# Four transformer layers in one kernel: where masks, forget rows, a table's spread and halves of tokens stand

## Chip, cores, metric

The kernel runs on one core of a Trainium2 chip. The metric is the device time in microseconds of one execution, median of three runs.

## The reference

512 tokens of width 1024 pass through a first block of two layers, then a second block of two layers; all is fp32. Cut to what matters here:

```python
# first block, each of 2 layers: h = x @ w_in, split into four branches
y_mla = causal attention of rms-normed, projected q and kv, with rope
y_sb  = stick breaking: A[t,s] = sigmoid(z) * prod_{s<j<t} (1 - sigmoid(z[t,j])), s < t only
y_fox = causal attention, logit[t,s] += c[t] - c[s], c = cumsum(log_sigmoid(forget))
y_mem = softmax attention over x's queries and a memory of 256 rows
merged = sum_n sigmoid(merge) * (branch_n * silu(gate_n)) @ w_branch[n]
x = layer_norm(alpha * x + merged @ w_out)
# second block, each of 2 layers: h = rms_norm(x); z = h @ w_in, four branches
A: q, k rms-normed per head, axial rope, full attention    B: rope, window of 128, sinks
C: neighbourhood attention with a table of biases (rpb)    D: rope, softmax1 - lam * softmax2, rms norm
x = x + (concat of branches * silu(gates)) @ w_out ; at the end rms_norm
```

## The kernel before

`plan()` runs when the program is built. It makes one list of steps (`put(kind, ...)`), and each of the five engine programs walks this list and executes the steps that concern it, so every engine's queue is in order and an instruction that waits holds all behind it. The planner sets the order: `alongside()` interleaves the attention of one branch (scores, turns by TensorE, products) with the projections ("fill") of the next, by estimates of their cost. Stages of a layer in the first block: mem, mla, sb, fox, merge and output, layer norm; in the second block: A, B, D, C, output, rms norm.

A matrix product in fp32 is three matmuls on parts of the operands (`xh,wl`, L1399; `xl,wh`, L1400; `xh,wh`, L1401): activations and weights are split into a high half, a cast on ScalarE (ACT), and a low half, a subtraction on VectorE (DVE) or GpSimd (POOL). `wload()` puts a weight's load on SyncE (SP), 1 MB or in pieces, double buffered: load j waits for the casts of j-2. `hold` in the planner's state delays casts of weights. ACT casts it (L1552), DVE (L1897) and POOL (L2300) make the low half in turn. Activations enter a layer token-major in four tiles of 128 tokens; `features()` turns a tile by TensorE (L1362) and ACT (L1563) and DVE (L1904) split it. `opened()` runs the first projection in two halves of 256 tokens, with the turn of tiles 2 and 3 between, so that the first half needs tiles 0 and 1 only.

Names that the change touches: `spread` writes the C branch's bias table (`zscr` in HBM, two DMAs of 1920 KB, L1577 on ACT), which `bias` reads much later and whose DMA the sticks step waits for as well; `normed` is the rms norm of mla's compressed q and kv (result on DVE, high half on ACT in L1653, low half on POOL); `sticks` on DVE is a scan (L2166), a mask of the diagonal block (L2169) and a product (L2172), twice per step; `foxrow` are two DVE instructions per head (L2035) that add the decay rows to fox's q and k; `newton` refines a reciprocal root in four small instructions (L1870 to L1876), `newton_wide` one of 128x512 (L1860 to L1866); `dmix` combines D's two softmaxes (L2151, L2153, L2156); `tabs` are the rope tables that SP loads (L2416) for the rope of A, B and D (L2212). `out_partial` (wo2a) is the output projection of three branches, the fill of the C stage: 4 weights x 4 tiles x 6 x 3 = 288 matmuls of 256 columns; `sum` after it adds the last branch (wo2b).

## Time and profile before

| what | value |
| --- | --- |
| three runs, us | 1534.04, 1537.66, 1539.85; median 1537.66 |
| the profiled execution's own time | 1534.89 us |
| its span, first to last instruction | 1533.1 us, TensorE clock granted 0.975 of full |
| busy: TensorE / VectorE / ScalarE / GpSimd | 92% / 57% / 46% / 24% |
| chain of work that ended last | PE 69%, DVE 17%, ACT 8% |

PE is the TensorE matmul, PEld its weight load; a "q" behind an engine's name is its queue, where DMAs are issued. "L12" is line 12 of the kernel. A bracket behind an instruction is the engine's idle time before it and what ended it. A granted clock of 1.00 is 2.4 GHz, 0.50 is 1.2 GHz.

### The profile page before, as it was taken

What the parts mean: (1) busy time and instruction counts of PE and PEld (TensorE: products, weight loads), DVE (VectorE), ACT (ScalarE), POOL (GpSimd) and SP (SyncE); (2) the same over time, 40 slices, a digit from 0 to 9 for tenths busy, and PEclk for the clock granted to TensorE, in tenths of its full rate; (3) what the DMA queues carried; (4) which work ended last, traced back from release to release, by engine and by line L of the source; (5) the groups of instructions that cost most, each with busy time, mean ns of one, the idle gap of its engine ahead of it and who ended that gap; (6) DMA issues with size and microseconds to landing.
All of it is one profiled execution on the core that took longest, in us unless ns stands there. A gap on an engine that the chain in (4) does not pass through costs nothing.

```text
span 1533.1 us, 21207 instructions
## 1 busy us (share of the span) xinstructions
PE 1413.1 (92%) x8026; PEld 1091.0 (71%) x8026; DVE 869.9 (57%) x1657; ACT 709.6 (46%) x1525; POOL 366.7 (24%) x265
## 2 busy tenths in 40 slices
PE   7999899999989999999997899988998899988997
PEld 6767576777977677777786766665776766665776
DVE  4555337467662553465577565457656465557655
ACT  3555345455234554455543454445444344445443
POOL 2232131245231322223541112320111112320111
PEclk9999999999999999999998899998999899998999
DMA  6413620225242221112263232511313332411311
GB/s 227 111 30 87 158 83 15 78 67 213 97 151 56 52 88 56 55 45 62 91 214 98 60 77 48 111 56 49 97 62 111 83 76 53 99 55 49 97 63 55
DMA packets 191121, 131.73 MB, mean 86 GB/s; under 512 B 91436, under 2 KB 181164, under 8 KB 191020
## 3 DMA queue, kind: packets, MB, share of 16 engines
q1 hardware_dynamic: 179534, 112.29, 26.3%
q10 hardware_dynamic: 11486, 18.09, 3.7%
q8 instruction: 64, 1.05, 0.3%
q14 instruction: 37, 0.30, 0.1%
HBM read 118.03 MB, written 12.32 MB: 85 GB/s over the span
## 4 chain that ended last, share of the span: by engine, by line
PE 69%; DVE 17%; ACT 8%; issue 3%; DMA 1%; ACTq 1%; POOL 0%; DVEq 0%; POOLq 0%
PE pb L1399 18%; PE pb L1400 16%; PE pb L1401 16%; PE pb L1477 6%; PE pb L1421 5%; PE pb L1455 4%; ACT prob L1533 3%; ACT wh L1552 2%; ACT tmp L1533 1%; DVE wl L1897 1%; DVE small L2143 1%; DVE prob L2156 1%; DVE xl L1904 1%; DVE scr L2166 1%; DMA wr<-w_out 1%
## 5 line engine op out<-in xcount | busy, mean ns | idle before, releaser
L2300 POOL TENSOR_TENSOR wl<-wr,wh 128x512 fp32r<-128x512 f32 x170 | 236.4, 1390 | 886.2 <-ACT wh L1552 882.8
L1399 PE MATMUL pb<-xh,wl 128*128 128x512 f32 (+1 forms) x832 | 350.9, 422 | 25.5 <-DVE xl L1904 21.9
L1400 PE MATMUL pb<-xl,wh 128*128 128x512 f32 (+1 forms) x832 | 321.7, 387 | 0.0
L1401 PE MATMUL pb<-xh,wh 128*128 128x512 f32 (+1 forms) x832 | 321.7, 387 | 0.0
L1897 DVE TENSOR_TENSOR wl<-wr,wh 128x512 fp32r<-128x512 f32 x200 | 161.1, 807 | 198.7 <-ACT wh L1552 198.4
L1399 PEld LDWEIGHTS pb<-xh,wl 128*128 128x128 f32 x832 | 162.0, 195 | 103.7 <-issue 50.1
L1552 ACT CAST wh<-wr 128x512 fp32r<-128x512 f32 x370 | 211.1, 603 | 29.3 <-PE pb L1401 23.8
L1401 PEld LDWEIGHTS pb<-xh,wh 128*128 128x128 f32 x832 | 161.7, 194 | 31.7
L1400 PEld LDWEIGHTS pb<-xl,wh 128*128 128x128 f32 x832 | 162.4, 195 | 24.3 <-issue 3.8
L1533 ACT ACTIVATE prob<-prob,small 128x512 f32<-128x512 f32 (+3 forms) x128 | 76.3, 596 | 148.5 <-DVE small L2120 139.1
L1455 PE MATMUL pb<-cst,prob 128*128 128x128 f32 x768 | 120.8, 279 | 22.3 <-ACT prob L1533 8.4
L1399 PE MATMUL pb<-wh,xl 128*128 128x256 f32 x448 | 130.0, 290 | 8.0 <-DVE xl L2062 3.5
L1455 PEld LDWEIGHTS pb<-cst,prob 128*128 128x128 f32 x768 | 95.2, 143 | 54.3 <-issue 14.6
L1400 PE MATMUL pb<-wl,xh 128*128 128x256 f32 x448 | 126.7, 283 | 0.0
L1401 PE MATMUL pb<-wh,xh 128*128 128x256 f32 x448 | 126.7, 283 | 0.0
L1533 ACT ACTIVATE tmp<-pb,cst 128x512 f32<-128x512 f32 (+3 forms) x128 | 82.6, 645 | 71.2 <-PE pb L1421 21.4
L1533 ACT ACTIVATE prob<-pb,small 128x512 f32<-128x512 f32 (+1 forms) x96 | 58.4, 611 | 111.4 <-DVE small L2107 57.8
L1399 PEld LDWEIGHTS pb<-wh,xl 128*128 128x128 f32 x448 | 85.7, 191 | 13.0 <-DVE xl L2062 4.3
L1780 ACT COPY prob<-pb 128x512 f32<-128x512 f32 (+3 forms) x128 | 61.4, 480 | 69.3 <-PE pb L1455 68.3
L1399 PE MATMUL pb<-wh,yl 128*128 128x256 f32 (+1 forms) x272 | 87.4, 321 | 2.5 <-DVE wl L1897 1.3
L2180 DVE COPY prob<-pb 128x512 f32<-128x512 f32 (+3 forms) x128 | 70.5, 551 | 31.3 <-PE pb L1455 30.8
L1400 PEld LDWEIGHTS pb<-wl,xh 128*128 128x128 f32 x448 | 85.8, 192 | 0.7 <-issue 0.5
(196 smaller groups left out, 2446.5 us busy)
## 6 DMA issues: line engine op xcount, KB each, us to landing
wr<-w_in SPq DMA_DIRECT2D x39, 1024.0 KB, 5.1
wr<-w_in SPq DMA_DIRECT2D x48, 256.0 KB, 4.6
wr<-w_out SPq DMA_DIRECT2D x10, 1024.0 KB, 6.4
wr<-w_branch SPq DMA_DIRECT2D x48, 128.0 KB, 2.3
x<-prob SPq DMA_DIRECT2D x12, 512.0 KB, 2.6
wr<-w_out SPq DMA_DIRECT2D x48, 128.0 KB, 2.9
wr<-w_mem_kv SPq DMA_DIRECT2D x4, 1024.0 KB, 5.6
prob<-x ACTq DMA_DIRECT2D x2, 2048.0 KB, 10.2
```

Of the source, the lines that this page charges most:

```text
L1399: e.matmul(ps, ll, rh, start=start, stop=False)
L1400: e.matmul(ps, lh, rl, start=False, stop=False)
L1401: t = e.matmul(ps, lh, rh, start=False, stop=stop)
L1421: t = e.matmul(bank(b)[:, 0:128 * (hi - lo)], lhs, rhs, start=True, stop=br != "mla")
L1455: t = e.transpose(bank(b)[:, c], probs(p)[:, c], C("ident"))
L1477: t = e.matmul(bank(b)[64 * half:64 * half + 64, lo:hi], v_[:, j, vc:vc + 64], turns(s["t"][half])[:, j, lo - 256 * ih:hi - 256 * ih], sta ...
L1533: return e.activation(o, i, f, bias=C("zero", 0, i.shape[0]) if bias is None else bias, scale=scale, **kw)
L1552: e.copy(wh[:, j % 2, c0:c1], wr[:, j % 2, c0:c1]).then_inc(w_hi.sem, w_hi.mark((j, c)))
L1780: t = e.copy(turns(t_)[:, lo:hi, 128 * i:128 * i + 128], bank(b)[:, 0:128 * (hi - lo)].rearrange("p (j c) -> p j c", c=128))
L1897: t = e.tensor_tensor(wl[:, j % 2, c0:c1], wr[:, j % 2, c0:c1], wh[:, j % 2, c0:c1].bitcast(F32), ALU.subtract)
L2180: t = e.tensor_copy(turns(t_)[:, lo:hi, 128 * i:128 * i + 128], bank(b)[:, 0:128 * (hi - lo)].rearrange("p (j c) -> p j c", c=128))
L2300: t = e.tensor_tensor(wl[:, j % 2, c0:c1], wr[:, j % 2, c0:c1], wh[:, j % 2, c0:c1].bitcast(F32), ALU.subtract)
```

## The change

1. The table's spread moves from ACT to SP and is split into eight DMAs of 15 rows, two behind each of the next four weight loads of layer 0's mla stage.
2. The sb scores' diagonal block gets its strict mask as a matmul (identity times a matrix of large negative numbers) that adds to the scores; DVE's L2169 and the mask in the scan go. Two 128x128 tiles for it are made once.
3. `foxrow` moves from DVE to ACT.
4. The high and low halves of the `normed` rows become a step of their own, `normhi`, put about 5 us of the planner's time later.
5. Layer 1 of the first block opens with halves too: only tile 3 is turned between them.
6. Each layer of the second block opens with the first halves of two weights, Ag and Aq, then tiles 2 and 3, then Ag's and Aq's second halves.
7. Of the output projection wo2a, tiles 2 and 3 of its last weight (36 matmuls of 256 columns) are left and run between the sums of tiles 1 and 2.
8. `newton` has three instructions and its first does not wait for ACT's root; `newton_wide` has three; `dmix` does both halves' small instructions in one and waits for both exps first.

On ACT's queue in layer 0's mla stage, before (`ls` is the lambda step, `prob` the scores, `wr`/`wh` a weight and its high half, `zscr` the table):

```order
L1533 ACTIVATE u<-pb,cst 128x512
L1533 ACTIVATE ls<-ls,cst 128x4
L1577 DMA zscr<-scr 3840x1x128 x2
L1533 ACTIVATE prob,small<-prob,small 128x512 x2
L1552 CAST wh<-wr 128x512 x2
L1780 COPY prob<-pb 128x3x128
```

And on SP's queue in the changed kernel, from the load of the small tables on:

```order
L2442 DMA scr<-rpb_c 60x31 x2
L2410 DMA wr<-w_in 128x8x256
L2448 DMA zscr<-scr 960x1x128 x2
L2410 DMA wr<-w_in 128x8x256
L2448 DMA zscr<-scr 960x1x128 x2
L2410 DMA wr<-w_in 128x8x256
L2448 DMA zscr<-scr 960x1x128 x2
L2410 DMA wr<-w_in 128x8x256
L2448 DMA zscr<-scr 960x1x128 x2
L2410 DMA wr<-w_in 128x8x256
```

Between the lambda's exp and the scores' exps nothing stands on ACT any more; SP, which had five loads in a row there, has two parts after each of the first four.

On ACT in the mem stage of layer 0, where the normed rows of q and kv (`setB`) are cast; before:

```order
L1533 ACTIVATE tmp<-setB,cst 128x512
L1653 CAST yh<-setB 128x512 x3
L1533 ACTIVATE prob,small<-pb,small 128x256 x2
L1552 CAST wh<-wr 128x512 x2
L1780 COPY prob<-pb 128x2x128
L1533 ACTIVATE tmp<-pb,cst 128x512
L1533 ACTIVATE tmp<-tmp,cst 128x512
L1533 ACTIVATE prob,small<-pb,small 128x256 x2
L1653 CAST yh<-setB 128x512 x2
L1780 COPY prob<-pb 128x2x128
```

And now:

```order
L1585 ACTIVATE tmp<-setB,cst 128x512
L1585 ACTIVATE prob,small<-pb,small 128x256 x2
L1604 CAST wh<-wr 128x512 x2
L1837 COPY prob<-pb 128x2x128
L1700 CAST yh<-setB 128x512 x3
L1585 ACTIVATE tmp<-pb,cst 128x512
L1585 ACTIVATE tmp<-tmp,cst 128x512
L1585 ACTIVATE prob,small<-pb,small 128x256 x2
L1837 COPY prob<-pb 128x2x128
L1604 CAST wh<-wr 128x512 x2
L1700 CAST yh<-setB 128x512 x2
```

The casts of the three q rows and of the two kv rows now stand behind the copies of the turned scores.

On SP at the second block's beginning (`x<-prob` stores a tile, 128x8x64 is a quarter of a weight); before:

```order
L2365 DMA wr<-w_in 128x8x64 x4
L2416 DMA tabs<-tables 128x512 x2
L2365 DMA wr<-w_in 128x8x64 x4
L2365 DMA wr<-w_in 128x8x256
```

And now:

```order
L2410 DMA wr<-w_in 128x8x64 x8
L2466 DMA tabs<-tables 128x512 x2
L2410 DMA wr<-w_in 128x8x256
L2410 DMA wr<-w_in 128x8x64 x4
```

The rope tables stand behind four more pieces of a weight than before.

The diff, the planner's part:

```diff
+            spread(2)
+    def spread(n):
+        for _ in range(n):
+            if st["spread"] in range(8):
+                put("spread", l=st["spread"] // 4, r=15 * (st["spread"] % 4))
+                st["spread"] += 1
...
+    def halves(w, ep, half, held):
+        for c in range(2):
+            drain(gemm("fm", w, 128 * c, 128 * c + 128, ("x", ep), range(8), n=256, b=held[c], off=256 * half,
+                       end=half == 1))
...
+        halves(w, ep, 0, held)
+        between()
+        halves(w, ep, 1, held)
...
+            ready = now() + 5000
+            for _ in range(40):
+                if now() < ready:
+                    yield
+            put("normhi", l=l, grp=grp)
...
+        rest_of(norm_q)
...
+        rest_of(norm_kv)
...
-        if l:
-            held = [drain(gemm("fm", w, 128 * c, 128 * c + 128, ("x", l), range(8))) for c in range(2)]
-        else:
-            held = opened(w, l, lambda: last_features(l, *X))
+        held = opened(w, l, lambda: last_features(l, X, (3,) if l else (2, 3)))
...
+            st["spread"] = 0
...
+            yield from proj_fm("sbq", l, "sb", "q", l, False)
             if l == 0:
                 put("lambdas")
-                put("spread")
-            yield from proj_fm("sbq", l, "sb", "q", l, False)
...
+        spread(8)
...
-            for turned in ((0, 1), (2,), (3,), ()):
+            for turned in ((0, 1), (2,), ()):
                 next(parts)
                 advance_late(late)
                 for i in turned:
                     run(features(1, i, (X[i],)))
             rest_of(parts)
-            give(*X)
+            while advance_late(late):
+                pass
...
-        for x in gate(br + "g", ep, br, l, (lambda: last_features(ep)) if br == "A" else None):
+        two, held = [None, None], [(), ()]
+        if br == "A":
+            two, held = [wnext(br + "g"), wnext(br + "q")], [[GR[0].take() for _ in range(2)] for _ in range(2)]
+            st["hold"] = True
+            for w, h in zip(two, held):
+                halves(w, ep, 0, h)
+            last_features(ep)
+            halves(two[0], ep, 1, held[0])
+        for x in gate(br + "g", ep, br, l, two[0], held[0]):
             if x is not None:
                 box["u"] = x
             yield
+        if br == "A":
+            st["hold"] = False
+            halves(two[1], ep, 1, held[1])
...
+        w = two[1] if br == "A" else wnext(br + "q")
...
+            if br == "A" and n < 2:
+                b = held[1][n]
+            else:
+                b = yield from beside(gemm("fm", w, c0, c0 + 128, ("x", ep), range(8)))
...
-            sq = TM.take() if br == "A" else None
+            sq = TA.take() if br == "A" else None
...
-            for i in range(4):
+            for i in range(2 if m == 3 else 4):
                 b = yield from gemm("tok", w, 0, 256, ("y2", l), range(4 if i in held else 0, 6), tile=i, b=held.get(i),
                                     start=i not in held)
                 put("acc", l=l, m=m, i=i, b=b)
                 give(b)
                 yield
-            wdone(w)
+            if m < 3:
+                wdone(w)
+        box["w"] = w
+    def out_left(l, w, i):
+        b = drain(gemm("tok", w, 0, 256, ("y2", l), range(6), tile=i))
+        put("acc", l=l, m=3, i=i, b=b)
+        give(b)
...
+        st["hold"] = True
...
+            if i == 2:
+                for n in (2, 3):
+                    out_left(l, box["w"], n)
+                    advance_late(late)
+                wdone(box["w"])
+                st["hold"] = False
...
```

TensorE's, ScalarE's and VectorE's parts (the code of `spread` and `foxrow` is otherwise what it was; SP now runs `e.dma_start(zscr[l][r], src)` for 15 rows `r`):

```diff
                         lhs, rhs = q_[:, 2 * c + half, ti], k_[:, 2 * c + half, tk]
                     else:
                         lhs, rhs = q_[r, c, ti], k_[r, c, tk]
-                    t = e.matmul(bank(b)[:, 0:128 * (hi - lo)], lhs, rhs, start=True, stop=br != "mla")
-                    if br != "mla":
+                    t = e.matmul(bank(b)[:, 0:128 * (hi - lo)], lhs, rhs, start=True, stop=br not in ("mla", "sb"))
+                    if br not in ("mla", "sb"):
+                        t.then_inc(logit.sem, logit.mark(b))
+                if br == "sb":
+                    w.wait_ge(v_fn, v_fn.at("masks"))
+                    for b in s["b"]:
+                        t = e.matmul(bank(b)[:, 128 * i:128 * i + 128], identr[:, :], strict[:, :], start=False, stop=True)
                         t.then_inc(logit.sem, logit.mark(b))
...
-            elif k == "spread":
-                for l in range(2):
-                    w.wait_ge(d_z, d_z.at("z"))
-                    src = zrow[:, l, :].unsqueeze(1).to_broadcast([60, 64, P])
-                    e.dma_start(zscr[l], src).then_inc(d_spread.sem, d_spread.mark("z"))
...
-            elif k == "normed":
+            elif k == "normhi":
...
+            elif k == "foxrow":
+                l, h = s["l"], s["h"]
+                w.wait_ge(v_fn, v_fn.at(("foxsum", l)))
+                w.wait_ge(p_fn, p_fn.at(("zeros", l)))
+                fa, fb = CONST_COLS["foxa"][0], CONST_COLS["foxb"][0]
+                p0 = 64 * (1 - h % 2)
+                for dst, n in ((QKV["fox"][0], 0), (QKV["fox"][1], 1 + h)):
+                    t = act(dst[p0:p0 + 36, h, :], fz[:, :], ACT.Identity, cst[0:36, fa + n:fa + n + 1],
+                            cst[0:36, fb + n:fb + n + 1])
+                    t.then_inc(a_copy.sem, a_copy.mark(("foxrow", l, h)))
...
             for g, n in tn.free():
                 w.wait_ge(g, n)
-            e.tensor_tensor(x, o, o, ALU.mult).then_inc(v_fn.sem, v_fn.mark())
+            e.scalar_tensor_tensor(x, v, dim * 1e-6, o, ALU.add, ALU.mult).then_inc(v_fn.sem, v_fn.mark())
             w.wait_ge(v_fn, v_fn.n)
-            e.scalar_tensor_tensor(x, v, dim * 1e-6, x, ALU.add, ALU.mult).then_inc(v_fn.sem, v_fn.mark())
+            e.scalar_tensor_tensor(x, x, -0.5 / dim, o, ALU.mult, ALU.mult).then_inc(v_fn.sem, v_fn.mark())
             w.wait_ge(v_fn, v_fn.n)
-            e.tensor_scalar(x, x, -0.5 / dim, 1.5, ALU.mult, ALU.add).then_inc(v_fn.sem, v_fn.mark())
+            e.scalar_tensor_tensor(o, x, 1.5, o, ALU.add, ALU.mult).then_inc(v_fn.sem, v_fn.mark(*key, ends=(tn,)))
             w.wait_ge(v_fn, v_fn.n)
-            e.tensor_tensor(o, o, x, ALU.mult).then_inc(v_fn.sem, v_fn.mark(*key, ends=(tn,)))
-            w.wait_ge(v_fn, v_fn.n)
-
-        def newton(rs, var, scale, eps, x, y):
-            e.tensor_scalar(y, var, scale, eps, ALU.mult, ALU.add).then_inc(v_fn.sem, v_fn.mark())
+        def newton(rs, var, scale, eps, x, y, root):
+            e.tensor_scalar(y, var, -0.5 * scale, -0.5 * eps, ALU.mult, ALU.add).then_inc(v_fn.sem, v_fn.mark())
+            w.wait_ge(a_fn, a_fn.at(root))
             w.wait_ge(v_fn, v_fn.n)
             e.scalar_tensor_tensor(x, rs, y, rs, ALU.mult, ALU.mult).then_inc(v_fn.sem, v_fn.mark())
             w.wait_ge(v_fn, v_fn.n)
-            e.tensor_scalar(x, x, -0.5, 1.5, ALU.mult, ALU.add).then_inc(v_fn.sem, v_fn.mark())
-            w.wait_ge(v_fn, v_fn.n)
...
                     t.then_inc(v_att.sem, v_att.mark(("max", b)))
             elif k == "dmix":
                 l, i = s["l"], s["i"]
+                first, ratio = (small[:, s["sm"].slot.i, c + i:c + i + 5:4] for c in (8, 24))
+                for use in s["ta"]:
+                    w.wait_ge(a_att, a_att.at(("exp", use)))
+                e.reciprocal(ratio, ratio).then_inc(v_att.sem, v_att.mark())
+                w.wait_ge(v_att, v_att.n)
+                t = e.scalar_tensor_tensor(ratio, ratio, lam[:, l:l + 1], first, ALU.mult, ALU.mult)
+                t.then_inc(v_att.sem, v_att.mark())
+                w.wait_ge(v_att, v_att.n)
                 for half in range(2):
-                    d, x, p, use = probs(s["e"][half]), 4 * half + i, s["e"][half], s["ta"][half]
-                    ratio = sm(s["sm"], 24 + x)
-                    w.wait_ge(a_att, a_att.at(("exp", use)))
-                    e.reciprocal(ratio, ratio).then_inc(v_att.sem, v_att.mark())
-                    w.wait_ge(v_att, v_att.n)
-                    t = e.scalar_tensor_tensor(ratio, ratio, lam[:, l:l + 1], sm(s["sm"], 8 + x), ALU.mult, ALU.mult)
-                    t.then_inc(v_att.sem, v_att.mark())
-                    w.wait_ge(v_att, v_att.n)
-                    t = e.scalar_tensor_tensor(d, tm(use), ratio, d, ALU.mult, ALU.add)
+                    d, p, use = probs(s["e"][half]), s["e"][half], s["ta"][half]
+                    t = e.scalar_tensor_tensor(d, tm(use), sm(s["sm"], 24 + 4 * half + i), d, ALU.mult, ALU.add)
                     t.then_inc(v_att.sem, v_att.mark(("mixed", p), ends=(use,)))
             elif k == "sticks":
                 n = 128 * (s["i"] + 1)
                 for p, use in zip(s["e"], s["ta"]):
                     w.wait_ge(d_spread, d_spread.at("z"))
-                    x, lo, d, dg = tm(use)[:, 0:n], tmpz[:, 0:n], probs(p)[:, 0:n], slice(n - 128, n)
+                    x, lo, d = tm(use)[:, 0:n], tmpz[:, 0:n], probs(p)[:, 0:n]
                     w.wait_ge(a_att, a_att.at(("keep", use)))
                     w.wait_ge(v_att, v_att.n)
-                    m = mask_cols("after", 512 - n, 512)
-                    t = e.tensor_tensor_scan(lo[:, ::-1], x[:, ::-1], m[:, ::-1], 1.0, ALU.mult, ALU.max)
+                    t = e.tensor_tensor_scan(lo[:, ::-1], x[:, ::-1], x[:, ::-1], 1.0, ALU.mult, ALU.bypass)
                     t.then_inc(v_att.sem, v_att.mark(ends=(use,)))
                     w.wait_ge(a_att, a_att.at(("break", p)))
-                    t = e.scalar_tensor_tensor(d[:, dg], mask_cols("after", 384, 512), 1.0, d[:, dg], ALU.is_lt, ALU.mult)
...
```

## Rows read from the trace of the kernel before

**Rows 1.** The page, part 1: busy us, share and instructions by engine.

```profile
PE 1413.1 (92%) x8026; PEld 1091.0 (71%) x8026; DVE 869.9 (57%) x1657; ACT 709.6 (46%) x1525; POOL 366.7 (24%) x265
```

**Rows 2.** Timeline of PE: start, us, instruction; brackets are idle before, and releaser.

```profile
109.94 1.08 PE L1477 MATMUL pb<-prob,tbias 128*64 128x256 f32 x8 [2.10 <-ACT prob L1780]
...
169.32 1.11 PE L1455 MATMUL pb<-cst,prob 128*128 128x128 f32 x4 [5.21 <-DVE prob L2180]
...
443.17 1.97 PE L1362 MATMUL pb<-cst,prob 128*128 128x128 f32 x8 [4.25 <-DVE prob L2087]
...
837.17 1.97 PE L1362 MATMUL pb<-cst,setB 128*128 128x128 f32 x8 [7.20 <-DVE stats L1870]
844.56 0.58 PE L1399 MATMUL pb<-xh,wl 128*128 128x256 f32 x1 [5.42 <-DVE xl L1904]
...
858.42 0.39 PE L1399 MATMUL pb<-xh,wl 128*128 128x256 f32 x1 [4.35 <-DVE xl L1904]
...
1191.55 0.58 PE L1399 MATMUL pb<-xh,wl 128*128 128x256 f32 x1 [8.36 <-DVE xl L1904]
```

**Rows 3.** Windows: length; PE, PEld, DVE, ACT, POOL busy; clock, DMA share, GB/s.

```profile
165.90:172.70 6.80, 3.38 (x10) 2.79 (x11) 3.17 (x9) 4.28 (x12) 1.27 (x1) 0.50 0.94 190
442.40:449.20 6.80, 6.03 (x28) 6.03 (x29) 2.69 (x4) 2.21 (x4) 1.28 (x1) 0.50 0.20 79
858.80:862.20 3.40, 3.40 (x19) 3.40 (x18) 0.00 (x0) 0.00 (x0) 0.00 (x0) 0.50 1.33 226
848.60:851.80 3.20, 3.20 (x28) 3.20 (x28) 1.15 (x5) 3.13 (x7) 0.15 (x1) 1.00 0.41 164
```

**Rows 4.** Timeline of ACT and its queue (ACTq) in layer 0's mla stage.

```profile
156.52 9.47 ACTq L1577 DMA_DIRECT2D zscr<-scr  x2
166.04 0.72 ACT L1533 ACTIVATE prob<-prob,small 128x512 f32<-128x512 f32 x1 [9.23 <-issue]
```

**Rows 5.** DMA: list of issues; line L1577 alone; timelines of SP's queue and ACT.

```profile
wr<-w_in SPq DMA_DIRECT2D x39, 1024.0 KB, 5.1
...
DMA to landing us min/median/max: 13.8/18.3/22.7
...
199.07 9.97 SPq L2365 DMA_DIRECT2D wr<-w_in  x2
...
213.62 1.14 ACT L1552 CAST wh<-wr 128x512 fp32r<-128x512 f32 x2
```

**Rows 6.** Lines L2169 and L2035: ns min, median, max; first and last start.

```profile
L2169 DVE SCALAR_TENSOR_TENSOR prob<-cst,prob x32: 254/267/1296, 221.2 to 675.1; 128x128 f32<-128x128 f32 x32
...
L2035 DVE TENSOR_SCALAR setA<-fz,cst x16: 530/532/1475, 234.5 to 669.9; 36x512 f32<-36x512 f32 x16
```

**Rows 7.** Waits of PE, 225 to 246: us in total, times, longest.

```profile
PE pb L1455 <- DVE prob L2172: 3.2, 3, 1.3
```

**Rows 8.** Timeline of PE in layer 0's D stage: eight 128x128 turns.

```profile
1030.50 1.03 PE L1455 MATMUL pb<-cst,prob 128*128 128x128 f32 x8
```

**Rows 9.** Timeline of the tail: PE's last matmul, DVE's last Newton step and product.

```profile
1523.82 0.39 PE L1401 MATMUL pb<-wh,yh 128*128 128x512 f32 x1
...
1527.89 0.15 DVE L1870 TENSOR_SCALAR stats<-stats 128x1 f32<-128x1 f32 x1
...
1528.71 1.28 DVE L2095 SCALAR_TENSOR_TENSOR prob<-prob,stats,scr 128x1024 f32<-128x1024 f32 x1
```

**Rows 10.** Timelines of SP's queue and DVE at the second block's start.

```profile
856.00 2.96 SPq L2365 DMA_DIRECT2D wr<-w_in  x4
859.01 1.61 SPq L2416 DMA_DIRECT2D tabs<-tables  x2
...
875.02 0.69 DVE L2212 TENSOR_TENSOR tmp<-pb,tabs 128x512 f32<-128x512 f32 x1 [0.99 <-PE pb L1508]
```

**Rows 11.** Windows, columns as in group 3: D stage, C stage.

```profile
1025.00:1050.00 25.00, 20.05 (x112) 13.23 (x105) 19.98 (x42) 13.01 (x34) 2.29 (x2) 0.93 0.14 43
...
1125.00:1150.00 25.00, 25.00 (x189) 19.74 (x185) 13.37 (x32) 11.04 (x25) 3.53 (x3) 1.00 0.12 43
```

61 lines of the change are left out of this document (25 added, 36 removed).

## The prediction

> **What bounds the kernel now.** I read the page's busy shares first. TensorE (PE) works 1413.1 of 1533.1 us, 92%, and no other engine comes near [rows 1]. So the kernel ends when PE's matmuls end, and a change can move the time in three ways only: by closing gaps in front of PE, by giving PE its higher clock (2.4 GHz) in a stretch where it had the lower (1.2 GHz), or by changing the number of PE's instructions. Next I read PE's timeline for bracketed idle times. Outside PE's busy time lie 1533.1 - 1413.1 = 120 us; the reader is to see in [rows 2] that the long ones stand at few places: after a two-layer block's or layer's beginning (443, 837, 844, 858, 1191), once in the mla stage of layer 0 (169), once in the mem stage (110), and then each names the engine that ended it. Then I read the granted clock over stretches [rows 3]: each long gap is followed by a stretch at 0.50, the lower level; so a gap costs its own length and then as much again as half of PE's busy time in the slow stretch. In 165.9 to 172.7, PE was busy 3.38 us at half clock, so 1.7 us were lost to the clock; in 442.4 to 449.2 it was 6.03, so 3.0; three other stretches (from 111.3, 230.8 and 858.8) are 3.40 long and full, 1.7 each, of which the last stands in the rows.
>
> The sum is made against the profiled execution's own 1534.9 us (a span of 1533.1), which stands 2.8 below the median of 1537.66. I take the sum off the median at the end. "Layer" numbers below are those of the kernel: two blocks with layers 0 and 1 each.
>
> **1. The table's spread leaves ScalarE.** ACT issued two DMAs that took its queue 9.47 us, and the exp that the softmax of the mla stage wanted stood behind them, idle 9.23 [rows 4]. PE's gap of 5.21 at 169.32 hangs on it: the matmul waited for DVE's copy, which waited for that exp. Without the two issues nothing else is late in that window (DVE, ACT and POOL are under half busy), so the gap goes whole, and with it the clock loss: 5.21 + 1.7 = **6.9**. On SP's side, eight parts go in pairs behind the next four weight loads. The two whole DMAs were both down 24.2 us after the first issue, so an eighth costs about 3 us of transfer and a pair 6. A weight load lands in 5.1 [rows 5]; behind a pair it would land in about 11, and the load issued at 199.07 has its cast at 213.62, 14.5 us after the issue, so the later landing still fits; two or three microseconds more would not. SP itself has nothing else to issue there. The last pair goes behind the load of 208.66 (199.07 + 9.97, less 0.37 of its own) and would be down at about 208.7 + 5.1 + 6 = 219.8; the first masked product of the sb stage is at 221.2 [rows 6], a scan earlier it must be there. Cost taken 0, bounds 0 to 2. A lower bound for the whole item is what happens if the parts hold loads up (rival C).
>
> The Trainium skill, "DMA: Bandwidth & Descriptors", "Issuing engines are not separate DMA queues", says that all engines' DMAs run on the same 16 DMA engines and that another issuer saves only the sequencer's time, "usually small relative to the DMA itself". By that the item would be worth little; here the trace disagrees in size, since that time is 9.47 us on ACT. Its first half, one shared set of engines, is what rival C rests on.
>
> **2. The high halves of the normed rows (new step "normhi").** In the mem stage ACT's casts of the normed rows wait for DVE's result, and behind them in ACT's queue stands the copy of the turned scores, for which PE had waited 2.10 at 109.94 [rows 2]. The same gap of 2.10 comes once more in layer 1, at 526.08. The change puts the casts behind that copy. Gain 2 x 2.10, and the low clock after the first gap, 111.3 to 114.7, with PE busy 3.40, gives 1.7 [rows 3]: **5.9**. The casts' users (q and kv projections) come over 10 us later, so nothing is newly late. Bounds 3 to 6.
>
> **3. The sb stage.** DVE loses the masking of the diagonal, 16 per layer of 0.267 us plus what lies between (0.33 start to start), 5.3 us per layer, and the fox rows, 8 per layer of 0.53 (0.65), 5.2 us [rows 6]; ACT takes the latter over. The stage's gaps, 4.25 us per layer, wait mostly for DVE's sticks products (3.2 of them in [rows 7]), and the DVE part in front of each product is shortened by one instruction of 0.33, a pair by 0.66. I take 2.5 of 4.25 per layer as closed, 5.0, and the clock loss after 230.8, 3.40 busy, 1.7 [rows 3]. PE pays 32 new mask matmuls of 128 columns. No row shows this kind exactly. Bounds: 0.06 each, half of the 256-column pace, 28 in 3.20 us or some 0.12 in the last row of [rows 3], and 0.13 each, the pace of the 128x128 turns (1.03 for 8) [rows 8]: 1.9 to 4.2 in all. I take 3.7, near the turns, because they are as narrow. Net **3**, from 0 to 6. ACT, about half busy in that stage, has place for eight fox rows of some 0.6, but each stands before exps of the same stage; that is the reason for the lower bound.
>
> The Trainium skill, "TensorE: Matmul & The Clock Gate", "Back-to-back issue gap", gives some 81 ns per 128-column matmul in a stream of weight loads and matmuls. By that page the masks would cost 2.6 us, an estimate, and item 3 would be 4 instead of 3; no row shows it.
>
> **4. Layer 1 of the first block.** PE waits 4.25 at 443.17 for tile 3's layer norm [rows 2]. Now the second part of the memory's projection and the first half of mem's q, 5.8 us of work (48 x 0.12), come before that tile is turned. The gap and the low clock go (4.25 + 3.0); what is new is that the second half of q wants the turned tile at once, with no work between: two casts on ACT and two subtractions on DVE, 2.6. Net **4.6**, from 2 to 7.
>
> **5. Start of the second block (820 to 900).** Three gaps, 7.20, 5.42 and 4.35 [rows 2]. The first two are DVE's chain of norms and are shortened only by the Newton steps: three instructions in place of four, the first before the wait, about 0.2 each (four take 0.82 before, 1527.89 to 1528.71 in [rows 9]), 8 in the chain, 1.6. Before the third now stands the first half of Aq, which takes two weight casts of DVE (3.44) out of the way: 4.35 becomes some 2.5, and the clock loss of 858.8 (3.40 busy) goes, 1.7. Against it Aq's own low halves make PE wait perhaps 1.8. That is 3.4. But SP now issues all eight pieces of two weights before the rope tables (`tabs`). Before, four pieces went out at 856.0, the tables at 859.0, and DVE wanted them at 875.0 [rows 10]. The last four pieces wait for buffers that Ag's second half frees; with their issue and landing the tables land about 880.7, where DVE, shortened, would ask at 877: 3.7 late. The wide Newton steps give back 0.7 for each of three in that chain. 3.4 - 3.7 + 2.1 is 1.8; with the order of these waits uncertain I take **1.7**, from -3 to 6.
>
> **6. Start of the second block's layer 1.** 36 matmuls (4.3 us) of the output projection that ran before the sums now run between the sums of tiles 1 and 2. So tiles 0 and 1 are normed earlier, and the gap of 8.36 at 1191.55 shrinks by 3.8. The late tables take 1.2 of it back, a third of their 3.7 in 5, since here the loads are issued while PE still works on the sums. Net **2.6**, from 0 to 6.
>
> **7. D stages.** PE is idle 4.95 in a window of 25 us there, for ACT's exps and DVE's copies, 13 us per layer in eight gaps, and DVE is busy 20 of 25 [rows 11]. The mix of two halves loses one reciprocal and one scaling out of two each; 8 mixes per layer lose 0.4 to 0.5 each, but now wait for both exps: in the timeline half of them start when the second exp has about 0.5 to go, so these gain nothing and the other four gain 0.5 on DVE. The wide Newton steps of D give some more. **3** for both layers, from 0 to 8.
>
> **8. Tail.** From PE's last matmul to DVE's last instruction are 5.8 us [rows 9]. One product in front of the sum (0.64) can be done earlier, and the Newton steps give 0.4, with some waiting in between: **1.4**, from 0.4.
>
> **9. C stages.** They lose the 36 matmuls of 4.3 us as filling, and the four parts of tiles split otherwise. PE has no gap at all there (25.00 of 25.00) [rows 11]. I charge **-1**.
>
> Sum 6.9 + 5.9 + 3 + 4.6 + 1.7 + 2.6 + 3 + 1.4 - 1 = 28.1. The execution of 1534.9 would be 1506.8, the median 1537.66 - 28 = **1510**.
>
> **Rivals.** **B, gains at the layers' beginnings only shift.** DVE's chain of norms and rope, not PE's supply of work, sets the end of the stages 4, 5, 6, and the tables come late twice. Then only 1, 2, 7, 8 and half of 4 stay: 6.9 + 5.9 + 3 + 1.4 + 2.3 - 1 = 18.5, **1519**. For it: 5.42, 4.35 and 8.36 are all ended by DVE [rows 2]. Against: the new work ahead of the turns needs nothing of the late tiles. **C, the spread's parts hold the loads up.** A pair is about 6 us of transfers between two loads of 5.1 [rows 5]. If it is 3 us in each of four loads plus the first sticks' wait, item 1 falls from 6.9 to -5, and the time is 1510 + 12 = **1522**. Against: a load's cast came 14.5 us after its issue. **D, slower: the C stage runs dry.** The C stage's filling falls from 288 matmuls to 252. If that makes C's waits like D's (13 us of gaps and about 5 of clock per layer), the cost is 36 us, and the time 1537.66 - 28 + 36 = **1546**. It decides if DVE's share in C (13.4 of 25) comes near D's (20 of 25) [rows 11], which nothing in the change does. **E, the change does not do what it says** in the clock's part: the low stretches stay where they are, though shorter gaps. Then 1.7 + 1.7 + 1.7 + 3.0 + 1.7 = 9.8 are missing, **1520**.
>
> **How the numbers follow.** Forecast as summed 0.62, B 0.13, C 0.1, E 0.1, D 0.05. Likeliest 1510. The range goes from 1500 (3 to 8 at their upper ends in part) to 1525 (B, C and E within). 0.5% is 7.7 us, about what a measurement of this kernel can tell from no change; faster than 1530 holds the forecast, B, C and E, less some room for several of them together: 0.89. Same 0.07, slower 0.04.
>
> **What would show it.** In the changed kernel's trace: no gap over 1 us near 165 to 170 and none at 110 and 526 (1, 2); the mask matmuls' spacing 0.06 to 0.13, sb gaps under 2 us per layer (3); no gap before the turn of tile 3 near 430, but one of 2 to 3 after it (4); DVE waiting for `tabs` by a DMA near 850 and again near 1170 (5, 6); D gaps 10 to 13 per layer (7). PE's busy time falls by 8 to 12 us, because less of it is at the low clock, though it has 32 matmuls more. The prediction is wrong if weight loads land over 10 us after issue with casts waiting for them, if low clock stretches move instead of going, or if gaps open in C.

## The result, and the profile after

The changed kernel took 1525.20 us (median of five runs, 1522.20 to 1528.83). The kernel before, run beside it, took 1539.85 (five runs, 1534.04 to 1542.09). The ratio is 0.9913 with a 95% interval of 0.9896 to 0.9930, so it is faster by about 13 us (0.9%). The forecast was 1510, with a range of 1500 to 1525: the direction was right, the size about half of what was forecast, and the time lies just above the range.

The profiled execution of the changed kernel took 1525.2 with a span of 1523.4, against 1534.89 and 1533.1. That is 9.7 us, less than the medians say, because the profiled execution of before was one of its quick ones. The page, part 1 (compare [rows 1]) and the chain that ended last:

```profile
PE 1418.6 (93%) x8202; PEld 1101.0 (72%) x8202; DVE 846.7 (56%) x1545; ACT 720.5 (47%) x1541; POOL 372.9 (24%) x265
...
PE 74%; DVE 12%; ACT 8%; issue 3%; DMA 2%; POOL 1%; SPq 1%; ACTq 0%; DVEq 0%; POOLq 0%
```

TensorE (PE) is busy 5.5 us longer than before, although the prediction had its busy time fall by 8 to 12 (its own terms give 9.8 less of low clock and 3.7 more for masks, a fall of 6.1). The last matmul of before started at 1523.82 [rows 9], that of after at 1515.42:

```profile
1515.42 0.39 PE L1448 MATMUL pb<-wh,yh 128*128 128x512 f32 x1
...
1518.35 0.15 DVE L1926 TENSOR_SCALAR stats<-stats 128x1 f32<-128x1 f32 x1
...
1519.05 1.29 DVE L2142 SCALAR_TENSOR_TENSOR prob<-prob,stats,scr 128x1024 f32<-128x1024 f32 x1
```

So a profile's span can be cut in four: PE's idle time up to its last matmul (the end of that matmul less PE's busy time), what the low clock cost (half of PE's busy time in the stretches at 0.50), the rest of the busy time, which is PE's work at full pace, and the tail after the last matmul. Worked out from the two pages and timelines:

| us | before | after | difference | the prediction's terms, added up by kind |
| --- | --- | --- | --- | --- |
| idle | 111.1 | 97.2 | -13.9 | -20.7 |
| low clock | 26.1 | 25.9 | -0.2 | -9.8 |
| work at full pace | 1387.1 | 1392.7 | +5.6 | +3.7 (masks) |
| tail after the last matmul | 8.9 | 7.6 | -1.3 | -1.4 |
| span | 1533.1 | 1523.4 | -9.7 | -28.1 |

Two thirds of the idle time that was to go went, and in sum nothing came back from the low clock. The extra work was 5.6 in place of 3.7. TensorE has 176 matmuls more than before (8202 against 8026): 32 are the masks, the other 144 come from splitting in two what was 512 columns wide (48 in layer 1 of the first block, 48 in each layer of the second), and the prediction had put nothing for them. The timeline of PE in the changed kernel, the rows that answer to [rows 2] (the turns and products after the same steps):

```profile
107.26 1.08 PE L1529 MATMUL pb<-prob,tbias 128*64 128x256 f32 x8
...
161.53 0.60 PE L1507 MATMUL pb<-cst,prob 128*128 128x128 f32 x4
...
823.44 1.97 PE L1409 MATMUL pb<-cst,setB 128*128 128x128 f32 x8 [6.78 <-DVE stats L1926]
830.65 0.58 PE L1446 MATMUL pb<-xh,wl 128*128 128x256 f32 x1 [5.24 <-DVE xl L1959]
...
839.75 0.39 PE L1446 MATMUL pb<-xh,wl 128*128 128x256 f32 x1 [1.61 <-DVE wl L1952]
...
849.67 0.39 PE L1446 MATMUL pb<-xh,wl 128*128 128x256 f32 x1 [1.88 <-DVE xl L1959]
...
876.49 1.12 PE L1560 MATMUL pb<-tmp,cst 128*128 128x512 f32 x2 [1.94 <-ACT tmp L1585]
882.01 0.63 PE L1577 MATMUL pb<-cst,tmp 128*128 128x128 f32 x4 [0.77 <-ACT tmp L1877]
883.46 0.50 PE L1446 MATMUL pb<-xh,wl 128*128 128x512 f32 x1 [0.83 <-DVE tmp L2257]
...
1178.66 0.55 PE L1446 MATMUL pb<-xh,wl 128*128 128x256 f32 x1 [8.06 <-issue]
```

The gaps of 2.10 and 5.21 have no bracket any more. The one of 4.25 is gone too, with two smaller ones in its place. The row at 876.49 has a new gap, and the long one of 8.36 is still 8.06.

Since both kernels run the same score matmuls and turns in the same order, the start of each can be set against its twin. The lead of the changed kernel, place by place (in profiled executions, so with whatever low clock each had):

| place | lead at its end | gained there | forecast |
| --- | --- | --- | --- |
| start | 0.5 | 0.5 | none |
| mem stages (casts of normed rows, both layers) | | 3.7 and 2.2 | 5.9 |
| mla stage of layer 0 (the spread) | 11.2 | 7.0 | 6.9 |
| sb stages | | 0.0 and -1.5 | 3 |
| merge, output, both layers | | -0.6 and -1.6 | none |
| start of the first block's layer 1 | 14.3 | 3.7 | 4.6 |
| start of the second block | 10.9 | -2.4 | 1.7 |
| A and B of layer 0 | 10.7 | -0.2 | none |
| D stages | | 1.0 and -0.3 | 3 |
| C stage, sums, start of layer 1 | 8.7 | -3.0 | 1.6 |
| B stage of layer 1 | 9.7 | 1.0 | none |
| C stage and sums of layer 1, then the tail | 9.7 | -1.0 and 1.3 | 1.4 |

The two edits that take something out of ScalarE's queue gave 12.9 us, as forecast within a tenth. The failures stand at the starts of the second block's layers (9 us short), in the sb stages (4.5 short), in the D stages (2.3) and in the merge and output stages (2.2, of which 1.6 is a low stretch at 769 that before does not have). Low clock is no separate place: it is in each of these.

### The profile page after: what moved, and what is told of

Read it like the earlier page. It is cut to its first block, busy times and chain, and to the rows that moved or that the text cites. A ratio compares the mean times of both kernels' runs of the same rounds, so it can differ in the third digit from the quotient of the medians.

```text
span 1523.4 us, 21528 instructions
## 1 busy us (share of the span) xinstructions
PE 1418.6 (93%) x8202; PEld 1101.0 (72%) x8202; DVE 846.7 (56%) x1545; ACT 720.5 (47%) x1541; POOL 372.9 (24%) x265
## 4 chain that ended last, share of the span: by engine, by line
PE 74%; DVE 12%; ACT 8%; issue 3%; DMA 2%; POOL 1%; SPq 1%; ACTq 0%; DVEq 0%; POOLq 0%
PE pb L1446 19%; PE pb L1448 17%; PE pb L1447 17%; PE pb L1529 6%; PE pb L1468 6%; PE pb L1507 4%; ACT prob L1585 2%; ACT tmp L1585 2%; ACT wh L1604 1%; DVE xl L1959 1%; DVE wl L1952 1%; PE pb L1491 1%; DVE prob L2204 1%; DMA wr<-w_out 1%; PE pb L1479 1%
## 5 line engine op out<-in xcount | busy, mean ns | idle before, releaser
L2345 POOL TENSOR_TENSOR wl<-wr,wh 128x512 fp32r<-128x512 f32 x170 | 242.8, 1428 | 879.7 <-ACT wh L1604 876.0
L1446 PE MATMUL pb<-xh,wl 128*128 128x512 f32 (+1 forms) x880 | 358.9, 408 | 26.5 <-DVE xl L1959 12.5
L1447 PE MATMUL pb<-xl,wh 128*128 128x512 f32 (+1 forms) x880 | 330.4, 376 | 0.0
L1448 PE MATMUL pb<-xh,wh 128*128 128x512 f32 (+1 forms) x880 | 330.4, 375 | 0.0
L1446 PEld LDWEIGHTS pb<-xh,wl 128*128 128x128 f32 x880 | 171.7, 195 | 99.2 <-issue 56.1
L1448 PEld LDWEIGHTS pb<-xh,wh 128*128 128x128 f32 x880 | 171.5, 195 | 29.8
L1447 PEld LDWEIGHTS pb<-xl,wh 128*128 128x128 f32 x880 | 172.4, 196 | 22.3 <-issue 3.6
L1585 ACT ACTIVATE prob<-prob,small 128x512 f32<-128x512 f32 (+3 forms) x128 | 76.3, 597 | 138.8 <-DVE small L2167 138.6
L1507 PEld LDWEIGHTS pb<-cst,prob 128*128 128x128 f32 x768 | 94.3, 142 | 42.2 <-issue 10.7
L1585 ACT ACTIVATE prob<-pb,small 128x512 f32<-128x512 f32 (+1 forms) x96 | 58.5, 612 | 117.3 <-DVE small L2154 64.8
L1585 ACT ACTIVATE tmp<-pb,cst 128x512 f32<-128x512 f32 (+3 forms) x128 | 82.5, 645 | 63.2 <-PE pb L1474 19.5
## 6 DMA issues: line engine op xcount, KB each, us to landing
prob<-x ACTq DMA_DIRECT2D x2, 2048.0 KB, 10.7
```

What stands on the lines that cost most here:

```text
L1446: e.matmul(ps, ll, rh, start=start, stop=False)
L1447: e.matmul(ps, lh, rl, start=False, stop=False)
L1448: t = e.matmul(ps, lh, rh, start=False, stop=stop)
L1507: t = e.transpose(bank(b)[:, c], probs(p)[:, c], C("ident"))
L1585: return e.activation(o, i, f, bias=C("zero", 0, i.shape[0]) if bias is None else bias, scale=scale, **kw)
L2345: t = e.tensor_tensor(wl[:, j % 2, c0:c1], wr[:, j % 2, c0:c1], wh[:, j % 2, c0:c1].bitcast(F32), ALU.subtract)
```

## Experiments

In all that follows "idle", "low clock" and "work" are the terms of the table above. One more thing has to be read with care: in some executions the first projection still ran at the lower pace (0.21 us from matmul to matmul in place of 0.12) until 16.4 to 17.2, in others only until 14.6 to 15.8, and where no stretch at 0.50 is listed in that first projection it shows only in the distance of matmuls. That is up to 3 us of "work" that says nothing on an edit. It is called a slow start below, and is taken off where work is compared.

### The tables first

```diff
         if br == "A":
+            put("tabs", l=l, br=br)
             two, held = [wnext(br + "g"), wnext(br + "q")], [[GR[0].take() for _ in range(2)] for _ in range(2)]
...
-        put("tabs", l=l, br=br)
+        if br != "A":
+            put("tabs", l=l, br=br)
```

> The changed kernel with one edit: in the A branch of the second block the rope tables are asked for before the two weights Ag and Aq, not behind their loads. Theory (late tables): in the changed kernel VectorE waits 4.9 us for the tables in each layer and the rope chain behind it opens TensorE's gaps of 1.94, 0.83 and 0.60 us. Then VectorE's wait for the tables is gone, TensorE's idle time between the second halves and A's first scores falls by 2 to 3 us per layer, and the time falls by 4 to 8 us from 1525. Rival (the two second halves keep ScalarE and VectorE busy anyway): the wait for the tables only turns into a wait for TensorE's turned rows, under 1 us per layer is gained, the time stays within 2 us of 1525.

Measured: 1517.15 us (five runs, 1513.08 to 1518.01) against 1537.59 for before (nine runs), ratio 0.9858 (0.9838 to 0.9878): 8 us below the changed kernel's median. In the changed kernel SyncE's queue and VectorE read:

```profile
841.42 23.68 SPq L2410 DMA_DIRECT2D wr<-w_in  x8
865.15 1.77 SPq L2466 DMA_DIRECT2D tabs<-tables  x2
...
870.46 0.69 DVE L2257 TENSOR_TENSOR tmp<-pb,tabs 128x512 f32<-128x512 f32 x1 [4.91 <-DMA tabs<-tables]
```

and the list of what VectorE waited for at the tile `tabs` (us in all, times) has

```profile
  DMA tabs<-tables: 9.8, 2
```

With the tables first, the timelines of SyncE's queue and of PE read:

```profile
836.59 2.24 SPq L2468 DMA_DIRECT2D tabs<-tables  x2
...
843.30 23.72 SPq L2412 DMA_DIRECT2D wr<-w_in  x8
...
881.67 0.63 PE L1579 MATMUL pb<-cst,tmp 128*128 128x128 f32 x4 [0.77 <-ACT tmp L1879]
```

The eight loads take their 23.7 us in both, because the last four pieces wait until casts are done that still use their buffer. What stands behind them is late, and the tables stood behind them. Of the gaps 1.94, 0.77 and 0.83 only the 0.77 is left. Idle fell from 97.2 to 93.6: by 3.4 and 1.9 at the two places, while 1.6 came back elsewhere. Low clock fell from 25.9 to 18.9 with four stretches fewer, and only the one at 1223 stood behind a gap that the edit closed (1.90 at 1222.39). The other three (769, 1025, 1370) stand at gaps that it does not touch, and why they went in this execution is open; so what is shown to be the edit's are 5.3 us of idle time and the 1.7 at 1223. The theory of the late tables holds; the prediction had named it, with 3.7 us late where 4.9 were measured, but had let the other gains outweigh it.

### Aq in full width

```diff
-            two, held = [wnext(br + "g"), wnext(br + "q")], [[GR[0].take() for _ in range(2)] for _ in range(2)]
-            st["hold"] = True
-            for w, h in zip(two, held):
-                halves(w, ep, 0, h)
-            last_features(ep)
-            halves(two[0], ep, 1, held[0])
+            two[0] = wnext(br + "g")
+            held[0] = opened(two[0], ep, lambda: last_features(ep))
...
```

> The changed kernel with Aq in full width after Ag, as in the kernel before; only Ag runs in halves. It has the early tables again, since only Ag's pieces are loaded ahead of them. Theory (late tables are the loss, the halves themselves gain): the span is 1 to 3 us shorter than the changed kernel's 1523.4, because the halves' gain of some 2 to 3 us per layer is lost but the tables' 3 to 4 come back. Rival (the halves cost by themselves, by their waits and by 48 more matmuls per layer): 4 to 6 us shorter. Second rival (the halves gain much more than late tables cost): longer by 2 or more.

Measured: 1519.45, span 1517.7, 5.7 us shorter than the changed kernel: the rival (the halves cost by themselves) has the size. Idle 94.1, low clock 22.9. But idle is within 0.5 of the run with the tables first, which keeps the halves. So the halves do not cost by waits of their own; without them the tables come early again. What the rival had right is the other part of its claim: with the slow start taken off, work is 1.5 us less than in the run with the tables first, for 96 matmuls fewer. A later run takes this up on the fastest kernel.

### Nothing left of the output projection

```diff
-            for i in range(2 if m == 3 else 4):
+            for i in range(4):
...
-            if i == 2:
-                for n in (2, 3):
-                    out_left(l, box["w"], n)
-                    advance_late(late)
...
```

> The changed kernel with all of the output projection wo2a in the C stage again, nothing left for between the sums. Theory (moving 36 matmuls shortens the long gap at the start of the second block's layer 1): TensorE's gap of 8.06 us before that layer's first projection grows by 3 to 4, the span is 2 to 4 us longer than 1523.4 for layer 0 and about 0 to 1 for layer 1's end. Rival (the gap only moved, what comes first of tiles 0 and 1 waits for tiles 2 and 3 anyway): the gap stays within 1 us, the span within 1 us.

Measured: span 1525.3, with the slow start that cost 2.5 of it; idle 98.3 against 97.2. The gap, from PE's timeline:

```profile
1180.74 0.58 PE L1437 MATMUL pb<-xh,wl 128*128 128x256 f32 x1 [8.32 <-DVE xl L1950]
```

8.32 against 8.06: the rival holds. Moving 36 matmuls between the sums shortened the gap behind them by 0.3 only. What else it did, read off this run: it closed the gap at the turn of the tiles before it (1.49 here, 1.69 in the kernel before, none in the changed kernel) and 1.3 in the rope stage behind it, and shortened the tail by 0.8; against that, the C stage has a new gap of 0.7. Idle time in all is 1.1 less.

### The tiles turned earlier

Why did it not? In the changed kernel the turn of tiles 0 and 1 is done at 1170.6. ScalarE's queue after it:

```profile
1171.25 1.15 ACT L1585 ACTIVATE prob<-prob,cst 128x1024 f32<-128x1024 f32 x1 [1.96 <-DVE prob L2322]
...
1173.05 0.60 ACT L1604 CAST wh<-wr 128x512 fp32r<-128x512 f32 x1
1173.56 2.04 ACT L1615 CAST xh<-pb 128x512 fp32r<-128x512 f32 x4
1175.47 3.24 ACT L1604 CAST wh<-wr 128x512 fp32r<-128x512 f32 x6
```

The turned tiles (`xh`) stand behind the squares of tile 3 (L1585), which wait for tile 3's sum. The edit, on top of the tables first, turns both tiles before tile 3's product:

```diff
             late.append(settle(i))
             advance_late(late)
             tick()
+            if i == 2 and l == 0:
+                for n in range(2):
+                    run(features(3, n))
+                    tick()
+                    tick()
...
-        if l == 0:
-            run(features(3, 0))
-            while advance_late(late):
-                pass
-            run(features(3, 1))
-        else:
+        if True:
```

> As the run with the tables first, and in addition tiles 0 and 1 of the second block's layer 1 are turned before tile 3's last product instead of behind it, with two weight casts after each. In the changed kernel TensorE turned these tiles at 1168.7, but ScalarE cast them only at 1173.6 behind tile 3's squares and VectorE at 1174.2, and the gap of 8.06 us stayed. Theory (the gap is an order of queues: the turned tiles stand behind tile 3's norm): the gap shrinks to 2 to 4 us, idle time falls by 4 to 6 us against the run with the tables first, the time to about 1512. Rival (the gap is held by the casts of the weight Ag, six of which end at 1178.7): it shrinks by at most 2 us, and the time stays at 1515 to 1517.

Measured: 1513.06 us (four runs, 1511.77 to 1515.92), ratio 0.9847 (0.9818 to 0.9876); idle 87.8 against 93.6, 5.8 less, of which 4.7 is this gap (8.05 to 3.40); low clock 19.0 against 18.9.

```profile
1162.33 1.91 PE L1411 MATMUL pb<-cst,setB 128*128 128x128 f32 x16
...
1170.40 0.36 PE L1448 MATMUL pb<-xh,wl 128*128 128x256 f32 x1 [3.40 <-issue]
```

The theory of the queue's order holds: the work of the change was right, its place in ScalarE's and VectorE's queues was not. The edit also puts casts of the next weight (`tick()`) right behind each turn; the gap shrank by more than the 2 us that the rival allowed, but what these casts alone give was not tried.

### Masks on VectorE again

```diff
-                    t = e.matmul(bank(b)[:, 0:128 * (hi - lo)], lhs, rhs, start=True, stop=br not in ("mla", "sb"))
+                    t = e.matmul(bank(b)[:, 0:128 * (hi - lo)], lhs, rhs, start=True, stop=br != "mla")
...
-                if br == "sb":
-                    w.wait_ge(v_fn, v_fn.at("masks"))
-                    for b in s["b"]:
-                        t = e.matmul(bank(b)[:, 128 * i:128 * i + 128], identr[:, :], strict[:, :], start=False, stop=True)
...
+                    t = e.scalar_tensor_tensor(d[:, dg], mask_cols("after", 384, 512), 1.0, d[:, dg], ALU.is_lt, ALU.mult)
...
```

> The changed kernel with VectorE masking the diagonal of the sb stage again (scan with a mask, one masked product of 128 columns each), and no mask matmuls; the forget rows stay on ScalarE. Theory (the mask matmuls cost TensorE about 0.11 us each, 1.76 per layer, as much as the shorter VectorE chain closes): TensorE's instructions fall by 32, its idle time in each sb stage grows by 1 to 2 us, the span is within 1.5 us of 1523.4. Rival (VectorE's chain has slack once the forget rows are gone): the gaps stay as in the changed kernel and the span is 3 to 4 us shorter. A low clock stretch more or less moves either by 1.7.

Measured: span 1522.9, in spite of the slow start (2.5). Idle 98.5 (+1.3), work less 3.2 when the start is taken off: 0.10 per mask. By stages, idle time grew by 1.7 and 1.4 in the two sb stages, as the theory had it, and fell by as much as 1.6 in one other place (the start of the second block) and 0.6 and 0.1 in the merge stages. In PE's timeline of the changed kernel a pair of masks stands between two other matmuls:

```profile
225.05 0.44 PE L1474 MATMUL pb<-strict,identr 128*128 128x128 f32 x2
225.32 0.45 PE L1446 MATMUL pb<-xh,wl 128*128 128x512 f32 x1
```

0.135 for one by start to start here. The theory holds for the sb stages: there the masks cost PE about what the shorter VectorE chain closes, 3.2 against 3.1.

On top of the early turn (with the same edit):

> The run before it, and the masks of the sb stage on VectorE again. Theory (masks are a loss of 1 to 2 us, 3.5 of matmuls against 1.3 of idle time, as the profile of that edit alone had it): 2 us shorter than the run before it. Rival (within noise): the same within 1 us.

Measured: 1508.70 us (four runs, 1505.66 to 1511.02), ratio 0.9821 (0.9787 to 0.9855), against 1513.06 without it: 4.4 less by medians whose ranges nearly touch. Idle in all is the same, 87.9, but not by stages: it grew by 1.3 in each sb stage, so the masks close gaps there in this kernel too, and it fell by 0.7 and 0.9 in the two merge stages and by 1.0 in other places. Work in the sb stages is lower by 3.4, 0.11 per mask.

The merge stages can be settled from the traces on record. In the changed kernel TensorE waits there for a low half of a weight by GpSimd:

```profile
364.68 0.36 PE L1446 MATMUL pb<-wh,xl 128*128 128x256 f32 x1 [0.45 <-POOL wl L2345]
```

A gap of this kind, 0.45 to 0.70 in layer 0 and 0.37 to 0.88 (once 3.06) in layer 1, stands in all seven profiles of kernels with the mask matmuls and in none of the seven without them. So the masks have a second price outside their own stage, 0.8 and 1.6 us for both layers by the two undoings; by what way they delay GpSimd is not shown.

### The forget rows on VectorE, and Aq in full width, on the fastest kernel

```diff
-                    t = act(dst[p0:p0 + 36, h, :], fz[:, :], ACT.Identity, cst[0:36, fa + n:fa + n + 1],
-                            cst[0:36, fb + n:fb + n + 1])
+                    t = e.tensor_scalar(dst[p0:p0 + 36, h, :], fz[:, :], cst[0:36, fa + n:fa + n + 1],
+                                        cst[0:36, fb + n:fb + n + 1], ALU.mult, ALU.add)
...
```

> The fastest kernel so far (tables first, early turn, masks on VectorE) with the forget rows on VectorE again as well, so that the sb stage is as before the change. Theory (the forget rows were what filled VectorE in front of the sticks products, and ScalarE has room): TensorE's idle time in the sb stages grows by 0.7 to 1.5 us per layer, the time by 1.5 to 3 from 1508.7. Rival (they cost ScalarE what they save VectorE): the same within 1 us.

Measured: 1509.40 us (four runs, 1507.05 to 1511.78), ratio 0.9816 (0.9794 to 0.9837). Idle 89.2, 1.3 more, of which 0.4 and 0.4 to 0.5 in the two sb stages. So neither theory quite: the rows on ScalarE save about 1 us of idle time, and the time shows no difference.

The other edit is that of "Aq in full width" on the same kernel:

> The fastest kernel so far (tables first, early turn, masks on VectorE) with Aq in full width after Ag in the second block, so that only Ag runs in halves, as before the change. Theory (once the tables are early the first half of Aq gives nothing, as the profile of the single edit had TensorE's idle time at 94.05 against 93.56): idle time within 1.5 us of 87.9, time within 2 us of 1508.7. Rival (the first half of Aq gives the 2 to 4 us that the prediction had for it, hidden so far by the tables): idle time 90 or more, time 1511 to 1514.

Measured: 1508.32 us (four runs, 1507.45 to 1509.70), ratio 0.9812 (0.9794 to 0.9830), idle 88.5. The theory holds: with the tables early the first half of Aq gives 0.6 us of idle time, and with slow starts taken off it costs 1.5 of work (96 matmuls more), the same as in the first pair. The time shows no difference. Its gaps:

```profile
827.03 0.58 PE L1438 MATMUL pb<-xh,wl 128*128 128x256 f32 x1 [5.24 <-DVE xl L1946]
...
840.24 0.38 PE L1438 MATMUL pb<-xh,wl 128*128 128x256 f32 x1 [3.21 <-DVE xl L1946]
```

3.21 in one gap, where the changed kernel has 1.61 and 1.88 in two.

### The spread alone, on the kernel before

```diff
+            st["spread"] = 0
...
-                put("spread")
...
-                    e.dma_start(zscr[l], src).then_inc(d_spread.sem, d_spread.mark("z"))
...
+                e.dma_start(zscr[l][r], src).then_inc(d_spread.sem, d_spread.mark("z"))
```

The first of the two DMA lines stood in ScalarE's program, the second is in SyncE's, with `r` one of eight parts.

> The kernel before with one part of the change: the table's spread on SyncE in eight parts. Theory (it removes the wait of ScalarE's queue and costs nothing): TensorE's idle time falls by 5.2 us from 111.1 to about 106, no gap near 165 to 170, the low clock after it goes or moves; span 5 to 8 us below 1533.1. Rival (the parts hold weight loads up): idle time falls by under 3 us and casts between 160 and 230 start later than before.

Measured: 1534.26, span 1532.4, only 0.7 below before. Yet the theory's core holds: idle 105.4, 5.7 less. In PE's timeline the row that answers to the one at 169.32 in [rows 2] has no gap, and SyncE's queue shows the longest pair of parts between two loads:

```profile
165.71 0.60 PE L1464 MATMUL pb<-cst,prob 128*128 128x128 f32 x4
```

```profile
203.44 0.38 SPq L2369 DMA_DIRECT2D wr<-w_in  x1
...
203.89 5.68 SPq L2407 DMA_DIRECT2D zscr<-scr  x2
...
221.83 0.39 SPq L2369 DMA_DIRECT2D wr<-w_in  x1
```

At 200 us it led before by 5.2 in spite of a start 1.8 behind. The rest went in low clock, 29.8 against 26.1 in this one execution, in new stretches at 521, 634 and 1201 that cost 1.7 each, all of them over 300 us behind the last part, at gaps that before has as well; why they stood there is open. The four pairs of parts held SyncE 1.94, 2.02, 2.18 and 5.68, and the next load was issued 12 us after the longest. The load between the last two pairs landed 8.9 us after its issue, where the prediction had reckoned 11, and TensorE's idle time shows no new gap there. Rival C is out.

### The Newton steps and D's mix as before

```diff
...
-            e.scalar_tensor_tensor(o, x, 1.5, o, ALU.add, ALU.mult).then_inc(v_fn.sem, v_fn.mark(*key, ends=(tn,)))
+            e.tensor_scalar(x, x, -0.5 / dim, 1.5, ALU.mult, ALU.add).then_inc(v_fn.sem, v_fn.mark())
+            w.wait_ge(v_fn, v_fn.n)
+            e.tensor_tensor(o, o, x, ALU.mult).then_inc(v_fn.sem, v_fn.mark(*key, ends=(tn,)))
...
```

(and the like in `newton` and `dmix`, as in the kernel before).

> The changed kernel with the Newton steps and D's mix as before. Theory (they were worth 3 us in the D stages and 2 to 3 elsewhere, as predicted): TensorE's idle time grows by 4 to 6 us from 97.2 and the end after its last matmul from 7.6 by 0.4. Rival (they shorten VectorE where something else ends the wait): idle time grows by under 2.5 us, in the D stages by under 1.5.

Measured: 1532.85, span 1531.1, of which 2.6 is a slow start; idle 101.7 against 97.2, 4.5 more, so the small steps are worth 4.5. They lie where the theory did not have most of them: about 1.4 at the second block's start, 0.9 in the D stage of layer 0 and none in that of layer 1, and 2.1 from the C stage to A's first scores in layer 1.

### Both kernels once more

> The kernel before, unchanged, profiled once more. Theory (where TensorE's low clock stands is partly chance of an execution, so a term of the sum that takes the low stretch behind one gap as gone is not to be had from one profile): TensorE's idle time is 111.1 us within 0.5 again, with the same gaps, while its low stretches stand at other places or have another total than 79.0 us by 3 or more. Rival (the low stretches follow from the gaps alone): the same places within a few us and the same total within 3.5.

> The changed kernel, unchanged, profiled once more. Same two theories: idle time 97.2 within 0.5 in both; by the first the stretches near 219.6, 622.4 and 769.2 are partly missing or elsewhere, by the rival all are there.

Measured: before 1534.56, span 1532.7, idle 109.9 (1.2 less, where 0.5 was expected), low stretches of 82.4 us in all against 79.0, at the same places, one of them longer. That total is 3.4 away, inside what the rival allowed and also what my theory asked for, so for the kernel before it decides nothing. After 1525.83, span 1524.0, idle 97.3, low stretches 70.1 us against 70.2. The changed kernel, first and second profile, by windows (columns as in [rows 3]):

```profile
367.10:373.90 6.80, 6.22 (x52) 6.01 (x52) 5.85 (x8) 3.26 (x6) 3.92 (x3) 1.00 0.47 154
622.40:625.80 3.40, 3.40 (x11) 2.17 (x11) 2.78 (x5) 1.90 (x3) 0.00 (x0) 0.50 0.00 0
```

```profile
622.90:626.30 3.40, 2.41 (x12) 1.93 (x13) 3.05 (x6) 2.72 (x6) 0.00 (x0) 1.00 0.14 45
367.10:373.90 6.80, 6.45 (x28) 6.16 (x29) 6.27 (x9) 3.25 (x6) 3.49 (x3) 0.50 0.47 154
```

The stretches after the long gaps stay. Those behind gaps of about a microsecond change: at 622 and 769 in the first execution, at 367 in the second. So my theory is right only for these, some 3.3 us of the cost, and the rival for the rest.

These moving stretches also say how far a line of the table of leads can be trusted. With the second pair of profiles the mla stage of layer 0 gains 7.1, the mem stages 3.7 and 2.1, the start of layer 1 3.7 and the start of the second block -2.2, as with the first. But the sb stage of layer 1 gives 0.1 in place of -1.5, and the merge stage of layer 0 -3.4 in place of -0.6.

## Why the prediction was off, point by point

In short, three kinds of term failed. Low clock: 9.8 us were booked as gone, 0.2 went. Idle time: 20.7 were booked, 13.9 went, chiefly because the rope tables and the turned tiles came late in their queues, and because the sb and D stages closed less. Work: 144 more matmuls were put at nothing and cost 2 to 3 us.

**Items 1 and 2** (6.9 and 5.9) came as worked out, 7.0 and 5.9, low clock included: the stretches after 110 and 169 are gone. (A small reading was off: in the first window of [rows 3] ScalarE is busy 4.28 of 6.80 us, over half and not under.) The Trainium skill's "Issuing engines are not separate DMA queues" ("DMA: Bandwidth & Descriptors") would have had the first near nothing; the run of this part alone, with 5.7 us less idle time, disagrees, for these two DMAs of 9.47 us in ScalarE's queue.

**Item 3** (3, measured -1.5). The price of the masks was near, 3.7 taken and 3.2 to 3.4 measured in the sb stages. The closing was not: idle time fell by 1.8 in each of the two stages, 3.5 where 5.0 were booked. The waits of 3.2 in [rows 7] are now

```profile
PE pb L1507 <- DVE prob L2217: 2.2, 3, 0.9
```

But the low clock after them stayed (at 220 instead of 231), and in one execution another came at 622. The failed steps are the closing, 1.5 short, and the clock term of 1.7 that was booked as gone, when gaps of 0.80 and 0.91 were still there. With the second pair of profiles, where none came at 622, the item is worth 0.1. The "Back-to-back issue gap" of "TensorE: Matmul & The Clock Gate" in the Trainium skill, 81 ns, was below what is measured here: 0.10 and 0.11 by two undoings, and 0.135 in the row.

**Item 4** (4.6, measured 3.7). The waits came as reckoned: the gap and its low stretch went, and gaps of 0.86 and 1.56 came in place of 2.6; idle time fell by 1.9 and low clock by 3.0. What is missing is work: this layer's first weight in halves has 48 matmuls more, and 1.3 us more of work stand here, a term that the prediction put at nothing.

**Item 5** (1.7, measured -2.4). The failed steps: the tables were 4.9 late, not 3.7; the low stretch at 859 was booked as gone, but a gap of 1.88 stayed there and so did the stretch, at 851; and Aq's 48 more matmuls, put at nothing, cost some 0.8 in this layer (1.5 in both). The first half of Aq, reckoned at nothing but its clock (1.85 less 1.8), gave 0.6 of idle time. The Newton steps, reckoned at 1.6 and 2.1, were worth 1.4.

**Items 6 and 9** (1.6 together, measured -3.0). The failed step is "tiles 0 and 1 are normed earlier, and the gap shrinks by 3.8". They were turned earlier, but ScalarE and VectorE, which had to take the turned rows, had tile 3's norm in their queues first. The order of ScalarE's instructions would have told it. Then the tables came 4.9 us late again, and a stretch of low clock came with that gap of 1.9, at 1223. Low clock around this start cost 5.2 where before had 2.6. The charge of 1 for the C stage was near: its new gap is 0.7.

**Item 7** (3, measured 0.7). The big waits in D did not change: those for the exp (3.09) not at all, the one of 3.50 by 0.4. The 3.09 is ended by ScalarE's exp, which a shorter mix does not make earlier.

**Item 8** (1.4, measured 1.3) was right.

**The rivals.** Neither C nor D came. B and E did, in part and together: B in the starts of the second block's layers, with the tables as its cause, and E in the low clock. Each alone had been priced at 1519 and 1520; both overlap in the forecast's terms of item 5. (B's sum also leaves out item 3, which is at no layer's beginning; with its 3 us B would stand at 1516.) The range ended at 1525 because no case held two rivals at once. That was the error of the range, as the clock term was that of the sum. Of the 9.8, the 6.4 behind gaps that vanished (110, 169, 443) came. The 3.4 at two places where gaps of 0.8 to 1.9 us stayed did not. And low clock that before does not have came to as much as was won: 1.7 at 622, 1.6 at 769, 2.6 around the start of the second block's layer 1, and the rest in small differences.

That a gap does not say by itself whether a low stretch follows stood in the profile of before already. The prediction says that each long gap is followed by one; but of the two equal gaps of 2.10, the one at 109.94 [rows 2] had one and the other had none, as the timeline and the window show:

```profile
526.08 1.08 PE L1477 MATMUL pb<-prob,tbias 128*64 128x256 f32 x8 [2.10 <-ACT prob L1780]
...
526.10:529.50 3.40, 3.40 (x19) 2.27 (x21) 0.69 (x1) 2.18 (x4) 3.24 (x3) 1.00 0.02 4
```

In the run of the spread alone this gap, unchanged, had one.

What is still open: the 0.45 before a low half of a weight by GpSimd, in the merge stage of layer 0, comes with the mask matmuls, but by what way is not shown. The start of the second block's first layer, where 6.78 and 5.24 wait for VectorE's chain, was not tried. And where low clock falls, beside the places that repeat in every profile, no run explains.

## What to carry to other kernels

When a step is moved, follow what it drags along on every queue: here the rope tables stood behind eight loads because a second weight was asked for earlier, and the turned tiles behind another tile's norm. A few lines each gave 8 and 4 us by the medians, nearly as much as the whole change. Book a gain from the clock only for a gap that goes entirely, and not as certain even then: in the run of the spread alone the stretch behind the closed gap went and three others came. Count the matmuls that a split adds. Put the cost of two rivals together into the range when they may come together. An edit that loads TensorE to relieve VectorE has to close more idle time than it adds work: the masks closed 2.7 to 3.1 us in their stages for 3.2 to 3.4 of work there and 0.8 to 1.6 of idle time in the merge stages, and the halves of Aq 0.6 for 1.5, and the fastest kernels (1508.7 and 1508.3, ratio 0.982 and 0.981) are without the masks, the second without those halves too.

## What the runs showed of the hardware

The low clock's cost does not follow the length of the gap before it. In the kernel before, 1.7 us were lost behind the gap of 5.21 and 3.0 behind that of 4.25; in the changed kernel 1.7 behind gaps of 0.80 and 0.91. A stretch of 3.4 us with PE busy throughout costs 1.7. Such stretches stood behind gaps of 0.80 to 1.20 in one execution of a kernel and not in the other (367, or 622 and 769). In both profiles of the changed kernel they stood behind the gap of 1.88 at 849.67 and not behind that of 1.94 at 876.49. The seven runs of before that went with the early turn had granted clocks of 0.977 at 1532.64 us and 0.972 at 1542.03: 0.005 of 1535 us would be 7.7 (an estimate from the rounded figures), most of a spread of 9. That is nearly as much as the 13 us that the change gave, so that one profile of each kernel tells gaps, but not the time. The DMAs of the spread held SyncE's queue 0.9 to 1.3 us for an eighth, but 2.8 for each of the last two, which were issued while the pair before was still in transfer. In the kernel before, ScalarE's queue was held 1.46 by the first whole one and 7.98 by the second, issued 1.5 us behind it:

```profile
L1577 ACTq DMA_DIRECT2D zscr<-scr x2: 1457/4718/7978, 156.5 to 158.0; - x2
```

So the time in the queue is not in proportion to what is moved; that it grows with what is still under way is a reading of these rows, and no run tried it alone.
